# Late modulation tiles, expert slots taken one by one, a decay clear moved, and two weight tiles that share their chunks

## The reference, cut to what matters

```python
# block 1
mod = silu(c) @ w_ada + b_ada                      # one row of 6 x 1024
sh1, sc1, gt1, sh2, sc2, gt2 = split(mod, 6)
h = rms_norm(x, g_pre_mix) * (1 + sc1) + sh1
y = hybrid_mixer(h, w_in, ..., w_out)              # window attention and gated linear attention
x = x + gt1 * rms_norm(y, g_post_mix)
h = rms_norm(x, g_pre_ffn) * (1 + sc2) + sh2
logits = h @ w_router + b_router                   # top 4 of 32, softmax over the four
y = sum over the four experts: gate * (swiglu(h @ w_mlp1[e] + b_mlp1[e]) @ w_mlp2[e] + b_mlp2[e])
x = x + gt2 * rms_norm(y, g_post_ffn)
# block 2: rmsnorm -> z = h @ w_in_2 -> three groups (the second, "hg", a decay recurrence) -> w_out_2,
#          conv_ffn, a gated projection, rmsnorm
# block 3: swiglu, chunked gmlp, swiglu, swiglu, nsa attention, swiglu, with layer norms between
```

## Time and profile before

| | |
|---|---|
| median of three runs | 2726.93 us (2722.19 to 2731.75) |
| the profiled execution | 2729.38 us |
| span of its trace | 2727.6 us, so 1.8 us lie outside the first and last instruction |
| PE busy | 2534.1 us (93%) |
| DVE busy | 1335.1 us (49%) |
| ACT busy | 908.5 us (33%) |
| POOL busy | 240.3 us (9%) |
| read from memory | 710.01 MB, 261 GB/s over the span |
| mean granted clock of PE | 0.965 of full |

### The profile page before, as it was taken

How to read it: one execution, slowest core, us unless ns; L and a number is a source line. 1 busy time by engine, 2 the same in 40 slices (tenths; PEclk the granted TensorE clock), 3 DMA queues, 4 the chain that set the end, 5 groups by cost and what they waited for, 6 DMA issues and landing times. The chain is left out here.

```text
span 2727.6 us, 39356 instructions
## 1 busy us (share of the span) xinstructions
PE 2534.1 (93%) x16728; PEld 1794.2 (66%) x16728; DVE 1335.1 (49%) x1869; ACT 908.5 (33%) x1236; POOL 240.3 (9%) x168
## 2 busy tenths in 40 slices
PE   7979899988999999778999899999999999999998
PEld 6752333332333333268799799998799999897897
DVE  4541122212212221278777765756665755765755
ACT  4431111111111111054555444454444444425443
POOL 3000000000000000011000101262020200102300
PEclk9989999999999999988999999999999999989999
DMA  9768999999999999943365566555466466441462
GB/s 325 241 237 368 427 428 405 428 427 428 428 416 409 428 427 428 380 140 109 129 205 195 167 211 214 164 179 186 155 213 206 155 204 205 147 143 46 156 210 99
DMA packets 248701, 713.71 MB, mean 262 GB/s; under 512 B 12531, under 2 KB 186313, under 8 KB 223622
## 3 DMA queue, kind: packets, MB, share of 16 engines
q1 hardware_dynamic: 237136, 690.26, 66.4%
q10 hardware_dynamic: 9734, 17.02, 1.9%
q0 software_dynamic: 1648, 3.82, 0.4%
HBM read 710.01 MB, written 1.05 MB: 261 GB/s over the span
## 5 line engine op out<-in xcount | busy, mean ns | idle before, releaser
L365 DVE TENSOR_TENSOR lo<-ring,hi 128x2048 fp32r<-128x2048 f32 x251 | 600.9, 2398 | 278.6 <-ACT hi L356 278.6
L356 ACT ACTIVATE hi<-ring 128x2048 fp32r<-128x2048 f32 x251 | 476.4, 1900 | 146.7 <-PE bank L653 114.0
L2020 PE MATMUL bank<-expert,xg 128*64 128x512 f32 x1664 | 396.5, 616 | 41.0 <-DMA expert<-in_w_mlp 40.0
L423 PE MATMUL bank<-x_hi,hi 128*128 128x256 f32 x1568 | 367.5, 279 | 0.0
L423 PE MATMUL bank<-x_lo,hi 128*128 128x256 f32 x1568 | 364.8, 278 | 0.0
L423 PEld LDWEIGHTS bank<-x_hi,hi 128*128 128x128 f32 x1568 | 295.1, 188 | 3.2 <-issue 1.6
L423 PEld LDWEIGHTS bank<-x_lo,hi 128*128 128x128 f32 x1568 | 295.0, 188 | 2.5 <-issue 1.0
L2020 PEld LDWEIGHTS bank<-expert,xg 128*64 128x64 f32 x1664 | 116.2, 140 | 256.9 <-issue 228.0
L2147 DVE TENSOR_TENSOR acc<-bank,acc 128x512 f32<-128x512 f32 x104 | 64.6, 683 | 325.1 <-PE bank L2128 325.1
L428 PE MATMUL bank<-x_hi,lo 128*128 128x256 f32 x1568 | 195.8, 278 | 0.0
L2103 PE MATMUL bank<-expert,aT 128*64 128x512 f32 x832 | 185.1, 596 | 4.9 <-DMA expert<-in_w_mlp 3.1
(11 more groups left out here) (650 smaller groups left out, 3827.2 us busy)
## 6 DMA issues: line engine op xcount, KB each, us to landing
expert<-in_w_mlp SPq DMA_DIRECT2D x192, 2048.0 KB, 18.8
ring<-in_l_ffn_w_in SPq DMA_DIRECT2D x88, 1024.0 KB, 5.0
ring<-in_l_ffn_w_out SPq DMA_DIRECT2D x44, 1024.0 KB, 4.8
ring<-in_w_ada SPq DMA_DIRECT2D x24, 1024.0 KB, 6.9
ring<-in_l_gm_w_in SPq DMA_DIRECT2D x24, 1024.0 KB, 5.2
ring<-in_ffn_w_up SPq DMA_DIRECT2D x22, 1024.0 KB, 5.0
ring<-in_w_in SPq DMA_DIRECT2D x21, 1024.0 KB, 7.4
ring<-in_l_gm_w_out SPq DMA_DIRECT2D x12, 1024.0 KB, 4.8
```

The costliest lines, as they stand in the source:

```text
L356: e.activation(k.half("hi", u), k.slot(j), ACT.Copy).then_inc(*k.up("hi_done"))
L365: e.tensor_tensor(k.half("lo", u), k.slot(k.units[u][0]), k.half("hi", u).bitcast(F32), SUB).then_inc(*k.up("lo_done"))
L423: e.matmul(o, l, r, start=fresh, stop=False, skip_group_check=True)
L2020: i = e.matmul(banks[n][j][h * CAP:(h + 1) * CAP, :], x, W[:, (2 * h + j) * 512:(2 * h + j + 1) * 512], start=c == 0, stop=False, skip_gro ...
```

## The change

- **Late tiles.** `LATE = (10, 11)`: the four loads of the two gt2 tiles now come behind the four `w_out` loads. Their products (`late_ada_pe`) go to four places: 10 h0 behind `w_out`, 10 h1 behind the turns to token order, 11 h0 behind the places, 11 h1 behind the turns of expert 0's tokens. The two flips go to expert 0, before part c = 2. The finish of gt2 leaves DVE: `late_gate_pool` on POOL issues two spreading transfers and runs an addition and a multiplication of 128x1024; `moe_out_dve` waits for it.
- **Turns.** `turned_pe` and `turned_dve` go from between the `w_out` units to expert 4, before part c = 5; the four parameter turns share one bank. The waits for the small inputs that stood ahead of them stand in `route_pe` and `route_dve`.
- **Expert slots.** `SLOTS = (3, 2, 4, 1, 0)`: load m goes into slot SLOTS[m modulo 5], and each of the first five waits only for what last used that place (`dense_left`).
- **Shared chunks.** `first_units_pe(ahead=True)` in all stages but the mixer: it waits for the hi of both units first, and on each chunk of the activation's hi runs unit 0 and unit 1.
- **Decay.** POOL clears the decay buffers behind the norm of block 2 (`mix2`, last unit), not as soon as the sums before it are there.

```diff
+SLOTS = (3, 2, 4, 1, 0)
...
     def expert_slot(self, m):
-        return self.t["expert"][:, m % NEXP, :]
+        return self.t["expert"][:, SLOTS[m % NEXP], :]
...
-def first_units_pe(k, e, banks, u0, toks, nm, xhi, xlo):
+def first_units_pe(k, e, banks, u0, toks, nm, xhi, xlo, ahead=True):
...
     e.wait_ge(*k.hi_at(u0))
-    product(0, "hi", xhi, first=True, each=lambda c: k.act(nm, "hi", c))
-    e.wait_ge(*k.lo_at(u0))
-    product(0, "lo", xhi)
-    e.wait_ge(*k.hi_at(u0 + 1))
-    product(1, "hi", xhi, first=True)
+    if ahead:
+        e.wait_ge(*k.hi_at(u0 + 1))
+        for c in range(8):
+            e.wait_ge(*k.act(nm, "hi", c))
+            for i in range(2):
+                chunk(i, "hi", xhi, c, c == 0)
+        e.wait_ge(*k.lo_at(u0))
+        product(0, "lo", xhi)
+    else:
...
+LATE = (10, 11)
+def late_ada_pe(k, e, i, h):
+    if h == 0:
+        k.bank(e, "ada", i, hold=True)
+    u, landed = k.raw_at(("ada", i, h))
+    e.wait_ge(*landed)
+    for q in range(4):
+        c = 4 * h + q
+        t = e.matmul(k.got("ada", i)[32 * q:32 * q + 32, :], k.t["sc"][:, c:c + 1].to_broadcast([128, 32]), u[:, q, :], start=h == 0, stop=h == 1, skip_group_check=True)
...
+def late_gate_pool(k, e):
+    g, bias, gain = k.t["g2"], k.t["unit"][:, 1, :], k.t["g1"]
+    e.wait_ge(*k.mm("pre2", "turn", 3))
+    for out, row in ((bias, k.A["b_ada"][0][5 * DM:6 * DM]), (gain, k.A["g_post_ffn"][0])):
+        e.dma_start(out, row.partition_broadcast(128)).then_inc(*k.up("g2_in", by=16))
+    e.wait_ge(*k.total("g2_in"))
+    e.wait_ge(*k.act("grow", LATE[-1]))
+    e.tensor_tensor(g, g, bias, ADD).then_inc(*k.POOL())
+    e.wait_ge(*k.pool())
+    e.tensor_tensor(g, g, gain, MUL).then_inc(*k.POOL("g2", "done"))
...
@@ mixer_out_pe
         rows_pe(k, e, "w_out", acc, k.first["w_out"] + n, pair(t["m_hi"], i), pair(t["m_lo"], i), n == 0, n == 3)
-        if n == 1:
-            turned_pe(k, e)
     acc_free(k, "w_out")
...
+    late_ada_pe(k, e, 10, 0)
...
@@ mixer_out_act
-    e.wait_ge(*k.dve("g2", "done"))
+    e.wait_ge(*k.dve("g1", "done"))
...
@@ the order of the loads
     for i in OUT_ORDER:
         k.unit("w_out", wview(k.A["w_out"][0])[:, 2 * i:2 * i + 2, :], 2, DM)
+    ada_units(k, LATE)
...
@@ route_pe
     bank = k.bank(e, "logits4")
+    e.wait_ge(*k.total("small_in"))
+    e.wait_ge(*k.total("b1_in"))
...
     to_tok_pe(k, e, "htok", t["x"])
+    late_ada_pe(k, e, 10, 1)
...
     m.then_inc(*k.MM("places"))
+    late_ada_pe(k, e, 11, 0)
...
         turn_x_pe(k, e, n)
+    late_ada_pe(k, e, 11, 1)
...
@@ route_rest_pe
+    elif c == 2:
+        for i in LATE:
+            late_flip_pe(k, e, i)
...
@@ experts_pe
+            if p == 4 and c == 5:
+                turned_pe(k, e)
...
+def dense_left(k, e, s):
+    if s < NSLOT // 2:
+        for j in range(k.last_load - NSLOT, k.last_load):
+            if j % NSLOT // 2 == s:
+                _, _, _, flag, key = k.loads[j]
+                e.wait_ge(*(k.lo_at(key) if flag == "lo_done" else k.at(flag, *key)))
+        return
+    halves = [(2 * s - NSLOT + i) % NP for i in range(2)]
+    e.wait_ge(*k.used(max(u for u in range(k.last_dense + 1) if u % NP in halves)))
 def experts_sp(k, e):
-    e.wait_ge(*k.lo_at(k.last_dense))
-    e.wait_ge(*k.used(k.last_dense))
...
+                else:
+                    dense_left(k, e, SLOTS[m])
...
@@ program_pool
-    for n in ("post1", "experts", "post2"):
+    meet(k, e, POOL_, "post1")
+    late_gate_pool(k, e)
+    for n in ("experts", "post2"):
         meet(k, e, POOL_, n)
+    e.wait_ge(*k.dve("mix2", "unit", 1, 1))
     decay_pool(k, e, "hg", k.t["hS"])
```

More of the change, by code:

```diff
@@ L610, in chain_dve, with chunk @@
     rms_unit_dve(k, e, then, 1)
-def first_units_pe(k, e, banks, u0, toks, nm, xhi, xlo):
+def first_units_pe(k, e, banks, u0, toks, nm, xhi, xlo, ahead=True):
+    def chunk(i, half, x, c, first=False, last=False):
+        for o, l, r in products(k, banks[i], k.half(half, u0 + i)[:, c, :], 256, (x[:, c, :],), toks[i]):
+            m = e.matmul(o, l, r, start=first, stop=last, skip_group_check=True)
+            first = False
+        return m
     def product(i, half, x, first=False, last=False, each=None):
-        w = k.half(half, u0 + i)
         for c in range(8):
@@ L619, in product @@
                 e.wait_ge(*each(c))
-            for o, l, r in products(k, banks[i], w[:, c, :], 256, (x[:, c, :],), toks[i]):
-                m = e.matmul(o, l, r, start=first, stop=last and c == 7, skip_group_check=True)
-                first = False
+            m = chunk(i, half, x, c, first and c == 0, last and c == 7)
         return m
     e.wait_ge(*k.hi_at(u0))
-    product(0, "hi", xhi, first=True, each=lambda c: k.act(nm, "hi", c))
-    e.wait_ge(*k.lo_at(u0))
-    product(0, "lo", xhi)
-    e.wait_ge(*k.hi_at(u0 + 1))
-    product(1, "hi", xhi, first=True)
+    if ahead:
[7 more added lines that the diff above has]
+    else:
+        product(0, "hi", xhi, first=True, each=lambda c: k.act(nm, "hi", c))
+        e.wait_ge(*k.lo_at(u0))
+        product(0, "lo", xhi)
+        e.wait_ge(*k.hi_at(u0 + 1))
+        product(1, "hi", xhi, first=True)
     product(0, "hi", xlo, last=True, each=lambda c: k.dve(nm, "lo", c // 2)).then_inc(*k.USED())
@@ L1028, with late_row, late_row_act, late_flip_pe @@
 ROW_TILES = {4: ("g1", 0), 5: ("g1", 1), 10: ("g2", 0), 11: ("g2", 1)}
+LATE = (10, 11)
+def late_row(k, i):
+    n, j = ROW_TILES[i]
+    return k.t[n][:, j * 512:(j + 1) * 512]
+def late_ada_pe(k, e, i, h):
[6 more added lines that the diff above has]
+        t = e.matmul(k.got("ada", i)[32 * q:32 * q + 32, :], k.t["sc"][:, c:c + 1].to_broadcast([128, 32]), u[:, q, :], start=h == 0, stop=h == 1, skip_group_check=True)
+    t.then_inc(*k.MM("ada", i, h))
+    if h == 1:
+        k.release("ada", i)
+def late_row_act(k, e, i):
+    e.wait_ge(*k.mm("ada", i, 1))
+    e.activation(late_row(k, i), k.got("ada", i)[:, :], ACT.Copy).then_inc(*k.ACT("ada", i, frees=("ada", i)))
+    k.past("act", ("ada", i, 1))
+def late_flip_pe(k, e, i):
+    bank = k.bank(e, "gate", i)
+    e.wait_ge(*k.act("ada", i))
+    e.matmul(bank[:, :], k.t["pick"], late_row(k, i)).then_inc(*k.MM("flip", i))
+def late_gate_pool(k, e):
[8 more added lines that the diff above has]
+    e.tensor_tensor(g, g, gain, MUL).then_inc(*k.POOL("g2", "done"))
 class Ticks:
@@ L1037, in __call__ @@
     def __call__(self, n):
-        for _ in range(min(n, 13 - self.next)):
+        for _ in range(min(n, LATE[0] + 1 - self.next)):
             self.step(self.k, self.e, self.next)
@@ L1112, in turned_pe @@
     t.then_inc(*k.MM("b1T"))
+    bank = k.bank(e, "late params")
     for g in (1, 2):
-        params_pe(k, e, g)
+        e.wait_ge(*k.total(f"params{g}"))
+        for i, rows in enumerate(k.plist[g][1]):
+            t = e.transpose(bank[:, (2 * g - 2 + i) * 128:(2 * g - 1 + i) * 128], rows, k.cc("ident"))
+    t.then_inc(*k.MM("late params"))
 def turned_dve(k, e):
-    e.wait_ge(*k.total("small_in"))
     e.wait_ge(*k.mm("b1T"))
     e.tensor_copy(flat(k.t["b1T"]), k.got("b1T")[:, :]).then_inc(*k.DVE(frees=("b1T",)))
+    e.wait_ge(*k.mm("late params"))
     for g in (1, 2):
-        params_dve(k, e, g)
+        inc = k.DVE("params", g, frees=("late params",) if g == 2 else None)
+        e.tensor_copy(k.plist[g][0], k.got("late params")[:, (g - 1) * 256:g * 256]).then_inc(*inc)
 IN_ORDER = (3, 4, 9, 0, 1, 2, 5, 6, 7, 8)
@@ L1190, in mixer_pe @@
     tick = Ticks(k, e, ada_next_pe)
-    first_units_pe(k, e, [k.bank(e, "w_in", n) for n in range(2)], u0, ((), ()), "pre1", t["m_hi"], t["m_lo"])
+    first_units_pe(k, e, [k.bank(e, "w_in", n) for n in range(2)], u0, ((), ()), "pre1", t["m_hi"], t["m_lo"], ahead=False)
     for n in (2, 3):
@@ L1228, in mixer_pe @@
     swa_values_pe(k, e, 2)
-    tick(2)
     k.release("mod")
@@ L2230, in experts_dve @@
                 scatter_dve(k, e, n)
+        if p == 4:
+            turned_dve(k, e)
         if p < NE:
@@ L3935, in program_sp @@
     experts_sp(k, e)
-    e.wait_ge(*k.expert_free(max(m for m in range(6 * NE) if 2 * (m % NEXP) < NSLOT)))
+    e.wait_ge(*k.expert_free(max(m for m in range(6 * NE) if 2 * SLOTS[m % NEXP] < NSLOT)))
     loads_sp(k, e, k.last_load, k.last_load + NSLOT)
```

27 lines of the change are left out of this document (15 added, 12 removed).

## The result

The changed kernel took 2715.5 us, median of six runs (2710.27 to 2717.54), beside 2729.3 us for the kernel before on the same chip: a ratio of 0.9949, 95% interval 0.9936 to 0.9962. On another chip it took 2713.2 us beside 2728.8, ratio 0.9940 (0.9921 to 0.9959). So it is 14 to 15.5 us faster; the forecast was 2710, 16.5 less, in a range of 2702 to 2719. The span of the trace went from 2727.6 to 2713.6 us.

A forecast was written before the change was run, and what follows sets the result against it. The chain through mixer, w_out, route and expert 0 was taken to set the experts' end. Mixer to experts -9.3, decay clear -2.4 and shared chunks -4.8 sum to -16.5 us: 2710, own bounds 2706 to 2715, with both rivals 2702 to 2719.

The forecast's parts named there:

- What bounds the kernel: Mixer to expert 0: the chain up to the load issued at 226.80 sets the experts' end one to one.
- `w_out` earlier and shorter: Mixer's end: start 7.3 us earlier, turns gone 3.6, slow products behind them 0.9; together 11.8 us gained.
- Half tiles in the route: Waits ahead of places, selection and expert 0: taken as 0, from -3.5 to +1.8 us.
- rival 1: Route: the clock stays up, selection and expert 0's first part at full clock, 3.5 us more gain, 2706.9; chance 0.20.
- The flips: Expert 0: two flips of gt2 on PE ahead of the release that counts cost 2.0 us in full.
- Finish of gt2 on POOL: Experts 0 and 1: POOL's addition and multiplication beside DVE's selection masks cost 0.5 us, from 0 to 2.
- Expert slots: First expert loads: issuing them one by one gains nothing, 0, at most 1 us either way.
- Turns in expert 4: Expert 4: PE's 3.6 us of turns are hidden where the queue is full; 0, at most 3.6.
- Clear behind the norm: Start of block 2: DVE's norm products no longer slowed by POOL's clears, -2.4 us, from -2.4 to -0.4.
- Openings: Seven stages other than block 2: unit 1's products fill unit 0's idle time, -4.8 us, from -8.5 to 0.
- rival 2: Route and openings: half tiles at lower clock cost 1.8 us, shared chunks gain 0, 2717.0; chance 0.20.

The follow-up runs named there:

- one_wait: The changed kernel with all first five expert loads waiting for everything that used their places: 2722.7 us, ratio 0.9985 to the kernel before.
- the two moves out of expert 0: The changed kernel with gt2's flips moved to expert 3: 2711.2 us, ratio 0.9925; then also the second bias's product moved to expert 2: 2709.6 us, ratio 0.9922.
- only_ahead: The kernel before with the interleaved openings alone, the mixer excepted: 2725.7 us, ratio 0.9993 (0.9979 to 1.0007).
- turns_back: The changed kernel with bias transposes and parameter turns back between w_out's second and third unit, the single bank kept: 2714.3 us, ratio 0.9952.
- no_fills: The changed kernel with all four late half tiles behind w_out, the three waits in the route empty again: 2715.1 us, ratio 0.9957.
- flips_later: The changed kernel with the two flips of gt2 in expert 3, not in expert 0: 2711.2 us, ratio 0.9925.
- clear_early: The changed kernel with POOL's clear of the decay buffers no longer waiting for block 2's norm: 2714.4 us, ratio 0.9951.

## Why the prediction was right, and where it was not

**What bounds the kernel: right.** Up to the first releases in expert 0 the chain sets the experts' end. `one_wait` delayed it and lost 9 us, the two moves out of expert 0 shortened it and the experts ended earlier by nearly as much.

**`w_out` earlier and shorter: right, and undersized.** 7.3 forecast for its start; the two traces of each kernel give 9.3 on the means, but starts of one kernel differ by 2 to 2.6 us, and the nine traces with the new order lie between 139.8 and 144.6. For the turns 3.6 + 0.9 was put down; `w_out` became shorter by 5.7 to 7.7. From unit to unit in the two traces before, the turns cost 3.7 and 3.8 us, the slow products behind them 1.0 and 2.7; the 0.9 was right in one trace and short in the other. A term that the sum does not have is `w_out`'s first unit, 1.1 to 1.3 us longer in the traces before (8.2 and 8.4, then 7.2 and 7.1) with more time at the lower clock. That part does not follow the edit: `only_ahead`, with the tiles and turns as before, took 7.0. `turns_back` shows 2.4 for turns put back where the clock stays up. The price of such small transposes depends on whether the clock falls behind them; why it falls in the traces before and not in `turns_back`, the wait for a bank or something else, is not shown.

**Half tiles in the route: the wrong case was taken.** I took 0 and gave rival 1 a chance of 0.20. Rival 1's mechanism came about, though not its time (2706.9): granted clock 1.00, selection and first part at 1.94 us. `no_fills` shows that the half tiles did it, 3.1 us worth in that pair of traces, beside 3.5 in the rival; in the second trace before only the selection was slow (3.28), so there they saved less. The flips cost more than their 2.0: 1.98 for themselves (at 196.66), and with the lower clock behind them 3.7 by `flips_later`. Expert 0 still came out at 39.3 us after 39.9 and 38.9, not 2.5 longer: up to its first down product it stood at the lower clock for 9 and 7 us before and for 3.4 after.

**Finish of gt2 on POOL: 0, not 0.5.** POOL and the next DVE instruction in the changed kernel:

```profile
199.43 2.34 POOL L1086 TENSOR_TENSOR g<-g,unit 128x1024 f32<-128x1024 f32 x1 [22.09 <-ACT g L1038]
201.85 2.34 POOL L1088 TENSOR_TENSOR g<-g,g 128x1024 f32<-128x1024 f32 x1
...
204.91 0.24 DVE L2003 TENSOR_SCALAR P<-early,posp 128x32 f32<-128x32 f32 x1 [8.28 <-ACT acc L1918]
```

DVE idles for 8.28 us there, waiting for ACT, so the two never met. The rule of the Trainium skill ("SBUF — State Buffer", "Who interferes with whom") that spoke against the move had nothing to act on at this place; no run here tests it for this pair.

**Expert slots: 0 was right only for the pair.** The prediction said that finer slots bring nothing. That held for expert 0's first product, but it did not see that the late tiles would hold up the first loads without them: 9 us in `one_wait`. The last expert load was issued 13.6 us earlier (1126.0, then 1112.4), not 9.

**Turns in expert 4: right.** From expert 0's first down product to the last one the experts took 906.1 to 907.4 us with the turns in `w_out` (four traces) and 906.4 to 907.9 with the turns in expert 4 and the slots as in the change or before (six traces). The three other traces with them there, `one_wait` and the two moves, have other lengths of expert 0 ahead of this stretch; they took 907.8 to 909.8. The queue stayed full around expert 4 in the changed kernel, a share of 1.01:

```profile
300.00:340.00 40.00, 39.86 (x199) 14.50 (x195) 10.10 (x23) 3.50 (x7) 0.00 (x0) 0.96 1.01 428
```

**Clear behind the norm: right, 2.0 and not 2.4**, by `clear_early`; the two traces of the kernel before lie 1.6 and 0.6 us over the changed kernel's in this stretch. The pair of DVE products fell to 0.88, and no split was held up: they took 2.29 beside the clears.

**Openings: the step that failed.** They became shorter by 5.5 us on the means (98.9 and 98.3 to 91.2 and 95.1), more than the 4.8 forecast. In `nsa`, from its first product to the first one by the activation's lo, it is 5.5 us, where it was 7.2 (from 2349.00 to the row here, then the two rows after):

```profile
2356.21 2.05 PE L621 MATMUL bank<-x_lo,hi 128*128 128x256 f32 x16
```

```profile
2333.39 3.88 PE L618 MATMUL bank<-x_hi,hi 128*128 128x256 f32 x32
...
2338.92 4.12 PE L618 MATMUL bank<-x_lo,hi 128*128 128x256 f32 x32
```

But the prediction took the gain at the opening as a gain of the stage. From opening to opening, `l0_ffn1` took 186.4 and 186.6 us before and 186.4 and 186.5 after; `gm` 229.5 before and 229.0 and 228.1 after; `l1_ffn1`, at the slower spacing, 191.4 and then 190.1 and 190.5. In `l0_ffn2` it came through, 188.1 and 187.2 before and 186.1 and 186.7 after. So part of the gain is lost again behind the opening; to what wait is not shown. Alone the openings moved the time by 1.9 us (-5.7 to +1.9).

**And a term that was not in the sum.** The part behind block 2's start differs by up to 12 us between traces, whatever the edit (1537.1 to 1549.2). Two things go with it: stages at the slower spacing, 4.2 us each, and time at the lower clock (82 to 109 us of this part). In the two pairs of traces it is the spacing: one and none such stages before, two and one after, 4.2 us more on the means, while the time at the lower clock was 4 us less. With 4.2 us taken off for each slow stage the part took 1538.6 and 1537.3 before, 1535.3 and 1538.9 after, 0.9 less on the means where 4.8 was forecast. So of the 8 us missing behind block 2's start, 4 went to the spacing and 4 are what the openings did not bring. The runs show that the spacing does not follow the edits one by one; what chooses the spacing of a stage was not found, and whether the changed kernel falls into the slower one more often than the kernel before stays open.

The forecast's time was thus right by two misses of opposite sign, which is luck: 6 too little in front, 8 too much behind. Of the 5.5 us between 2710 and 2715.5, 2.4 are its base: it counted from 2726.9, and the kernel before took 2729.3 beside the changed one. 2715.5 lies just outside the forecast's own bounds of 2706 to 2715, and the nearest time on record is rival 2's 2717.0; of its two halves, the slow half tiles did not come, and the chunks without gain nearly did.

What single parts are worth in time stays open. With the openings, the half tiles, the turns or the clear undone the kernel took 2714.3 to 2715.2, between the changed kernel's 2713.2 and 2715.5, though the traces show 2.0 to 3.1 us lost at the place of each of the last three.

Two slips stand in the working. A half tile of 1.9 us in a wait of 1.39 costs 0.5, not 1.0, and rival 1 with chunks gaining 8.5 comes to 2703, not 2702. The seven single gains behind the -4.8 are not given, so that term can't be followed stage by stage. None of this changes the forecast.

## What to carry to other kernels

Put short products into the waits of a latency-bound stretch on PE when they have to run anyway: here they paid twice, once for their old place and once by keeping the clock up. Where a stream of transfers follows, shorten what stands before its first releases, move what is not needed there behind them, and give each transfer only the wait of its own place. A gain at the opening of a stage counts only from that opening to the next, and edits of 2 to 4 us are to be read at their place in the trace when runs of one kernel spread by 9.

## What the runs showed of the hardware that was not expected

- At a granted clock of 1.00 a stream of 128x256 products ran at 0.113 or at 0.118 us each, for whole stages, in the same kernel at different runs: 4.2 us for a stage of some 1050 products.
- Small transposes between large products in `w_out` cost more than themselves where the clock fell behind them: 3.7 and 3.8 us, waits of 0.6 and 0.9 for a bank among them, and then 1.0 and 2.7 more in the unit behind (two traces before), against 2.5 and 0.1 where it stayed up (`turns_back`). `w_out` stood at the lower clock for 9 and 13 us in those two, and for 3.0 to 3.4 in every trace in which it took 23.6 to 26.4.
- POOL's clears, which only write, slowed DVE's normalising products from 0.88 us to between 2.57 and 3.24 for the first pair (four traces), but a DVE split beside them kept its 2.29.
